# A Mamba-2 mixer blocked between token tiles, one decay matrix for both directions, and a new order of work

## What is computed

```python
def ssd_chunked(xs, dt, a_coef, bm, cm):          # 2 chunks of 128 tokens, 8 groups of 4 heads of 64
    a_cs = jnp.cumsum(a, axis=1)                  # a = dt * a_coef
    decay = exp(where(lower, a_cs[l] - a_cs[s], -inf))
    cb = einsum('clgn,csgn->clsg', cc, bc)
    y_diag = einsum('clsg,clsgk,csgkp->clgkp', cb, decay, xdt)
    ...                                           # the state carried from chunk to chunk gives y_off
y = y_fwd + y_bwd + d_skip[:, None] * xs          # y_bwd: the same on the flipped sequence
y = grouped_rmsnorm(y * silu(z)) @ w_out
```

## Time and profile before

| | |
|---|---|
| median of 3 runs | 1599.66 us (1599.23 to 1608.36) |
| the profiled execution | 1603.29 us, span 1601.5 us |
| mean granted TensorE clock | 0.968 |
| busy: PE, DVE, ACT, POOL | 94%, 63%, 48%, 18% |
| DMA | 275 MB at 172 GB/s |
| from the first matmul of the layer's own units to its last, SSD layer 0 | 13.45 to 307.95 us |
| the same, SSD layer 3 | 1113.4 to 1405.8 us |

### The profile page before, as it was taken

How to read it: one execution, slowest core, us unless ns; L and a number is a source line. 1 busy time by engine, 2 the same in 40 slices (tenths; PEclk the granted TensorE clock), 3 DMA queues, 4 the chain that set the end, 5 groups by cost and what they waited for, 6 DMA issues and landing times.

```text
span 1601.5 us, 25464 instructions
## 1 busy us (share of the span) xinstructions
PE 1510.0 (94%) x10189; PEld 1400.4 (87%) x10189; DVE 1007.5 (63%) x1123; ACT 769.8 (48%) x1079; POOL 288.1 (18%) x357
## 2 busy tenths in 40 slices
PE   6989999899998999999999999999989998899998
PEld 6989888699987989999899889998889998789996
DVE  4768886655467566545744465556778788565545
ACT  3566666344443334444355535442566766435441
POOL 1334443162220000000000000000244343200000
PEclk9989999999999999999999999999989999899999
DMA  8736753366766464555454246555665465336552
GB/s 252 213 118 177 198 191 134 106 178 195 224 199 203 143 202 138 181 208 189 160 192 140 84 132 210 194 175 169 199 206 171 146 199 167 122 106 205 187 187 79
DMA packets 200757, 275.43 MB, mean 172 GB/s; under 512 B 12280, under 2 KB 168336, under 8 KB 200640
## 3 DMA queue, kind: packets, MB, share of 16 engines
q1 hardware_dynamic: 188032, 237.53, 45.0%
q0 software_dynamic: 11760, 35.94, 8.3%
q10 hardware_dynamic: 848, 0.32, 0.1%
HBM read 272.58 MB, written 1.18 MB: 171 GB/s over the span
## 4 chain that ended last, share of the span: by engine, by line
PE 49%; DVE 8%; ACT 3%; issue 2%; POOL 1%; DMA 0%; DVEq 0%; ACTq 0%; POOLq 0%
PE y L680 20%; PE acc L556 17%; PE acc L569 6%; PE inner L816 3%; DVE conv L1461 2%; DVE w_low L1333 2%; ACT w_high L995 2%; PE y L569 1%; DVE E L1495 1%; ACT E L1089 0%; PE y L913 0%; DMA E<-cumsum_dram 0%; DVE xT L1394 0%; PE inner L646 0%; DVE gate L1510 0%
## 5 line engine op out<-in xcount | busy, mean ns | idle before, releaser
L556 PE MATMUL acc<-xT,w_high 128*128 128x256 f32 x3328 | 617.0, 287 | 3.5 <-DVE ring_c L1473 2.7
L1333 DVE TENSOR_TENSOR w_low<-raw,w_high 128x2048 fp32r<-128x2048 f32 x226 | 518.9, 2306 | 154.0 <-ACT w_high L995 136.0
L556 PEld LDWEIGHTS acc<-xT,w_high 128*128 128x128 f32 x3328 | 531.4, 195 | 10.3 <-DVE ring_c L1473 3.4
L995 ACT ACTIVATE w_high<-raw 128x2048 fp32r<-128x2048 f32 x226 | 426.8, 1897 | 214.1 <-PE y L680 78.5
L556 PE MATMUL acc<-xT,w_low 128*128 128x256 f32 x1664 | 475.0, 285 | 0.0
L680 PE MATMUL y<-w_high,opT 128*128 128x512 f32 x1408 | 404.0, 396 | 15.3 <-DVE opT L1481 12.2
L680 PEld LDWEIGHTS y<-w_high,opT 128*128 128x128 f32 x1408 | 262.4, 190 | 70.6 <-issue 19.3
L556 PEld LDWEIGHTS acc<-xT,w_low 128*128 128x128 f32 x1664 | 323.8, 195 | 0.0
L680 PE MATMUL y<-w_low,opT 128*128 128x512 f32 x704 | 225.0, 393 | 0.0
L1349 DVE TENSOR_TENSOR opT<-conv,opT 128x512 fp32r<-128x512 f32 x56 | 39.3, 702 | 270.5 <-issue 246.2
L569 PE MATMUL acc<-w_high,xT 128*128 128x256 f32 (+1 forms) x960 | 182.6, 292 | 9.8 <-DVE xT L1394 9.3
(11 more groups left out here) (168 smaller groups left out, 1212.6 us busy)
## 6 DMA issues: line engine op xcount, KB each, us to landing
raw<-in_ffn_w_in SPq DMA_DIRECT2D x128, 512.0 KB, 4.7
raw<-in_ffn_w_out SPq DMA_DIRECT2D x128, 512.0 KB, 4.5
raw<-in_ssd_w_in SPq DMA_DIRECT2D x96, 512.0 KB, 5.4
E<-cumsum_dram POOLq DMA_DIRECT2D x32, 512.0 KB, 5.9
raw<-in_ssd_w_out SPq DMA_DIRECT2D x32, 512.0 KB, 5.4
raw<-in_sc_w_in SPq DMA_DIRECT2D x24, 512.0 KB, 4.6
raw<-in_na_w_qkv SPq DMA_DIRECT2D x24, 512.0 KB, 4.6
E<-cumsum_dram POOLq DMA_DIRECT2D x32, 256.0 KB, 6.3
```

The costliest lines, as they stand in the source:

```text
L556: mm = nc.tensor.matmul(bank[:, c * SEQ:(c + 1) * SEQ][:, span], w[:, col:col + P], xT[:, k, low, span], start=(k == 0 and part == 0), sto ...
L995: nc.scalar.activation(w_high[:, u % SPLIT, 0:k * c], raw[:, u % RAW, 0:k * c], ACT.Copy).then_inc(w_high_done, 1)
L1333: V.tensor_tensor(w_low[:, u % SPLIT, 0:k * c], raw[:, u % RAW, 0:k * c], f(w_high[:, u % SPLIT, 0:k * c]), ALU.subtract).then_inc(w_low_d ...
```

## The change

Between the two token tiles nothing depends on the pair of tokens but the score: so the far block is now the plain score (copied by ACT, `copy_cross`) times x scaled by its decay to the tile's end (`scale_xs`), two matmuls of 256 columns a group (`cross_chunk`), and DVE multiplies the result by the decay from the end and adds it (`add_cross`). Within a tile, forward decay stands in one triangle and backward decay in the other of one matrix: ACT shifts the backward half by a bias (`shift_decays`, 8 instructions), DVE joins the triangles (`join_decays`), ACT takes 8 exponentials in place of 16, DVE multiplies once. dt goes into the exponent as its logarithm, so x isn't scaled for the scan, and the scan is 8 matmuls a group. The diagonal lacks one direction; DVE sums the scores' diagonal and makes a factor for x (`own_token`), which takes the skip along, and POOL multiplies (`own_xs`). The DMAs of E are two a group, the selects are gone.

The order is new on all engines: the scan of a group comes one iteration earlier on PE, `dt` is ahead of z, and the time constants are ahead of the first silu. In the convolution layer PE projects cc and ch for the first token tile before the second has come (`features` with 128 columns), and each output unit comes one step later. x is loaded ahead of the weights.

```diff
@@ -78,10 +79,10 @@
         names = {}
         if kind == "ssd":
             for g in range(G + 2):
+                if g == 0:
+                    add(names, "dt", j, 0)
                 if g < G - 1:
                     add(names, "z", j, g)
-                if g == 0:
-                    add(names, "dt", j, 0)
...
         elif kind == "conv":
-            for b in range(5):
-                if b < 4:
-                    for what in ("cc", "ch", "cb"):
-                        add(names, what, j, b)
-                if b >= 1:
-                    add(names, "co", j, b - 1)
+            for b in range(4):
+                for what in ("cc", "ch", "cb"):
+                    add(names, what, j, b)
+                if b == 2:
+                    add(names, "co", j, 0)
+            for b in range(1, 4):
+                add(names, "co", j, b)
...
         def ahead_of_norm(s, t):
-            if t and s + 1 < len(subs) and subs[s + 1][0] == "ssd":
+            if t and s + 1 < len(subs) and subs[s + 1][0] in ("ssd", "conv"):
...
         @block.sync
         def _(sp):
+            for t in range(NT):
+                sp.dma_start(xs[:, t, :], x[0, t * P:(t + 1) * P, :]).then_inc(x_landed[t], 16)
             for u in range(len(units)):
-                if u < NT:
-                    sp.dma_start(xs[:, u, :], x[0, u * P:(u + 1) * P, :]).then_inc(x_landed[u], 16)
...
-                    def mask_decays(g):
...
-                        for q, (off, sign) in enumerate(((0, 1), (256, -1), (384 + P, -1), (640, 1))):
-                            v = slot[:, :, off:off + P]
-                            ins = nc.gpsimd.affine_select(out=v, in_=v, compare_op=ALU.is_ge, fill=GONE, base=0,
-                                                          pattern=[[0, HPG], [sign, P]], channel_multiplier=-sign)
-                        ins.then_inc(e_masked, 1)
+                        for d in range(2):
+                            src = rows[d * HEADS + g * HPG:d * HEADS + (g + 1) * HPG, :]
+                            src = bass.AP(src.tensor, src.offset, [[0, P], [1, HPG * SEQ]])
+                            pool.dma_start(decay_slot(n)[:, d * HPG * SEQ:(d + 1) * HPG * SEQ], src).then_inc(e_landed[n % 2], 16)
...
+                    def own_xs(g):
                         n = first + g
-                        pool.wait_ge(xs_scaled, n + 1)
-                        times_heads(tri_b[:, n % 2, :], n, spread(skip[:, j, g * HPG:(g + 1) * HPG],
-                                                                  [[0, NT], [1, HPG], [0, HD]])).then_inc(xs_skip, 1)
+                        pool.wait_ge(own_done, n + 1)
+                        if n:
+                            pool.wait_ge(off_added, n)
+                        times_heads(xs_own, n, spread(own_token[:, n % 2, 0, :],
+                                                      [[HPG, NT], [1, HPG], [0, HD]])).then_inc(xs_skip, 1)
...
-                    for g in range(G - 1):
+                    pool.wait_ge(ends_done, first // G + 1)
+                    for g in range(G):
                         scale_xs(g)
-                        if g >= 1:
-                            rms_power(g - 1)
-                            load_decays(g + 1)
-                        skip_xs(g)
-                        if g >= 1:
-                            mask_decays(g + 1)
-                    scale_xs(G - 1)
-                    rms_power(G - 2)
-                    skip_xs(G - 1)
-                    rms_power(G - 1)
+                        own_xs(g)
+                        if g + 2 < G:
+                            load_decays(g + 2)
+                        rms_power(g)
...
-                    head_units(s, [names[("z", 0)], names[("dt", 0)]])
+                    head_units(s, [names[("dt", 0)], names[("z", 0)]])
...
+                    def cross_chunk(g):
+                        m = n0 + g
+                        pe.wait_ge(cb_copied, m + 1)
+                        pe.wait_ge(xs_scaled, m + 1)
+                        bank = inner_bank(("off", m), (off_scaled, m + 1))
+                        for t in range(NT):
+                            mm = nc.tensor.matmul(bank[:, t * GW:(t + 1) * GW], cross[m % 2][:, (1 - t) * P:(2 - t) * P],
+                                                  xs_end[:, (1 - t) * GW:(2 - t) * GW], start=True, stop=True)
+                        mm.then_inc(off_ready, 1)
...
-                                             (1, ((P, xs_fwd, c0), (640, xs_fwd, c1), (384 + P, xs_bwd, c1)))):
-                                for q, (c, v, cv) in enumerate(terms):
-                                    mm = nc.tensor.matmul(bank[:, t * GW + h * HD:t * GW + (h + 1) * HD],
-                                                          e[:, c:c + P], v[:, cv:cv + HD], start=(q == 0), stop=(q == 2))
+                            for t in range(NT):
+                                c = t * GW + h * HD
+                                mm = nc.tensor.matmul(bank[:, c:c + HD], decay_slot(m)[:, h * SEQ + t * P:h * SEQ + (t + 1) * P],
+                                                      tri_b[:, m % 2, c:c + HD], start=True, stop=True)
...
-                    for i in range(1, G - 1):
-                        project(names[("z", i)], range(NT))
-                        if i <= 2:
-                            project(names[("bc", i)], range(NT))
+                    for i in range(1, G):
+                        if i < G - 1:
+                            project(names[("z", i)], range(NT))
+                        state_products(i - 1)
                         turn_xs(i - 1)
-                        if i >= 2:
-                            scan(i - 2)
-                        state_products(i - 1)
-                        if i > 2:
-                            project(names[("bc", i)], range(NT))
-                        if i > 2:
-                            turn_gated(i - 2)
+                        project(names[("bc", i)], range(NT))
+                        cross_chunk(i - 1)
+                        scan(i - 1)
                         project(names[("x", i)], range(NT))
-                        if i == 2:
-                            turn_gated(i - 2)
-                        if i >= 2:
-                            out_unit(s, names[("so", i - 2)], first=(i == 2))
-                    project(names[("bc", G - 1)], range(NT))
-                    turn_xs(G - 2)
-                    scan(G - 3)
-                    state_products(G - 2)
-                    project(names[("x", G - 1)], range(NT))
-                    turn_gated(G - 3)
+                        if i < G - 1:
+                            if i >= 2:
+                                out_unit(s, names[("so", i - 2)], first=(i == 2))
+                            turn_gated(i - 1)
...
                 elif kind == "conv":
-                    head_units(s, [])
-                    for b in range(5):
-                        if b < 4:
-                            project(names[("cc", b)], range(NT), arriving=None if b else (s, NT - 1))
+                    head_units(s, [names[("cc", 0)], names[("ch", 0)]])
+                    for b in range(4):
+                        if b:
+                            project(names[("cc", b)], range(NT))
                             project(names[("ch", b)], range(NT))
-                            project(names[("cb", b)], range(NT))
-                        if 1 <= b < 3:
-                            out_unit(s, names[("co", b - 1)], first=(b == 1))
+                        project(names[("cb", b)], range(NT))
+                        if b >= 2:
+                            out_unit(s, names[("co", b - 2)], first=(b == 2))
...
+                    def shift_decays(g):
+                        m = n0 + g
+                        act.wait_ge(e_landed[m % 2], 32 * (m // 2 + 1))
+                        for h in range(HPG):
+                            for t in range(NT):
+                                c = HPG * SEQ + h * SEQ + t * P
+                                e = decay_slot(m)[:, c:c + P]
+                                ins = nc.scalar.activation(e, e, ACT.Identity, bias=apart[:, t, g * HPG + h:g * HPG + h + 1])
+                        ins.then_inc(e_shifted, 1)
...
+                            for t in range(NT):
+                                e = decay_slot(m)[:, h * SEQ + t * P:h * SEQ + (t + 1) * P]
+                                ins = nc.scalar.activation(e, e, ACT.Exp, bias=ncs[:, t, g * HPG + h:g * HPG + h + 1])
...
+                    def copy_cross(g):
+                        m = n0 + g
+                        act.wait_ge(cb_ready, m + 1)
...
+                    act.wait_ge(dt_floor, mixer + 1)
+                    nc.scalar.activation(dtt[:, 6, :, :], dtt[:, 7, :, :], ACT.Ln).then_inc(dt_log, 1)
+                    z_tanh(0)
...
+                    for i in range(1, G):
+                        if i < G - 1:
+                            z_tanh(i)
```

(81 more changed lines are left out.)

195 lines of the change are left out of this document (78 added, 117 removed).

## The result

The changed kernel takes 1647.4 us (median of 4, 1645.9 to 1648.5) where the kernel before takes 1599.5: ratio 1.0278, 95% interval 1.0247 to 1.0309. It is 2.8% slower. The forecast was 1614.0, 0.9% slower, with 1641 as its upper end: the direction was right, the size was not. The profiled executions have spans of 1644.6 and 1601.5 us, a difference of 43.1.

A forecast was written before the change was run, and what follows sets the result against it. A loop of hand-overs between PE, DVE and ACT bounds the SSD iteration: 31.8 us, 33.4 with the clock. 1601.5 + 2 x 9.0 (mixers) - 6 + 3 (convolution) - 2 (start) = 1614.5, taken as 1614.0 us; range 1578 to 1641.

The forecast's parts named there:

- The loop: SSD iteration: PE, DVE and ACT hand-overs through turn_xs's wait for gated_low and add_cross take 31.8 us, against 32.0 before.
- Rival 3: SSD iteration: splits are done in time, PE bounds it at 28.5 us without stall; kernel 1552 us, chance 0.15.
- The clock: SSD iteration: the slow clock behind PE's wait of about 4.2 us at turn_xs costs 1.6 us a group.
- The upper bound of 3.1: SSD iteration: the most that the slow clock behind the stall was taken to cost, 3.1 us a group.
- The end of the mixer: SSD mixer, from scan 6 through the last output unit: 43.2 us at full clock.
- The start of the mixer: SSD mixer: the first scan comes 10.5 us sooner.
- The convolution layer: Convolution layer: -6 us at its end, where co1 fills PE's stall, and +3 at its start.
- Rival 2: Convolution layer's start: matmuls of 128 columns run at the plain float32 rate, 220 ns; kernel 1634 us, chance 0.2.
- DVE and ACT even: SSD iteration: DVE's 1.5 us more a group offset by POOL's selects gone; ACT half a microsecond less.
- the start of the program: Layer 0: x loaded ahead of the weights and dt's smaller load save 2 us.

The follow-up runs named there:

- Run 1: Changed kernel with the gated operand's two instructions (ACT and DVE) ahead of the weight split in each steady iteration: 1593.9 us, 0.9973 of the kernel before.
- run 3: Changed kernel with extra, never-read matmuls on PE ahead of turn_xs, in the stall: 1622.7 us, 1.0127 of the kernel before.
- run 6: Changed kernel with the order of DVE and ACT in the SSD mixers written anew: 1547.6 us, 0.9652 of the kernel before.
- Run 11: Changed kernel with only the last gated operand of each SSD mixer put ahead of the last split: 1646.3 us, 1.0277 of the kernel before.
- Run 8: Kernel before with only the new convolution layer put in: 1599.0 us, 0.9972 of the kernel before.
- run 2: Changed kernel with the gated operand right behind start_conv of x on ACT and ahead of the taps of x on DVE: 1594.7 us, 0.9985.
- run 10: run 7 with instructions added on PE, DVE and ACT whose results are never read: 1588.3 us.
- run 7: run 6 with the counter of small PSUM results raised by 4 ahead of the attention layer: 1539.3 us, 0.9621 of the kernel before.

## Why the prediction was wrong in size and right in kind

Four steps of the sum failed: the price of the clock behind a stall, the end of the mixer, where the splits were left out, and two terms that it put at nothing, the attention layer and the end of the program. The loop itself was right.

**The loop** held. The odd number of small results, the wait at `turn_xs` for `gated_low`, and the loop through `add_cross` are in the trace, 4.20 us at each steady stall (9.93 and 7.45 at the last two). Run 1 shows the cause: with the operand ahead of the split the stall is 1.44 us and the iteration 30.3. Its sum of 31.8 us measured 31.5 in run 3. Rival 3, the broken loop, needed another order on ACT and DVE; run 6 shows it at 27.1 us.

**The clock** was the first mis-sized term. 1.6 us was taken from the earlier trace rows, the cheapest of three stalls; it measured 2.4. The length of the wait didn't tell the price: behind 4.26 us before the clock was at half for some 3.4 us (0.63 over 4 us and 0.95 over the next 4), behind 4.20 us here for 5.4. And the stall of 3.01 us was read too cheap: its window of 4 us ended before the clock was back, and the next 4 us (595 to 599, clock 0.77) lost 0.9 us more, so 2.9 and not 2.0. With 31.5 that gives the 33.9 us, against 33.4. The six iterations from the first scan to the seventh (1189.18 to 1393.30) took 204.1 us, 3.7 us a mixer more than forecast: 6 x 0.8 for the clock, less 6 x 0.3 for the loop, and 0.7 for iterations a little longer than 33.9. The upper bound of 3.1 held.

**The end of the mixer** was the second: 43.2 us from the seventh scan, and 1.6 for the clock, against 50.4. Three of its terms were short. Transposes to scan of group 7: 6.0 against 8.7 us, because half an output unit, at half clock, stands between `turn_xs` and the cross product. The gate to the operand: 6.5 against 9.3, because a split stands ahead of it on ACT and on DVE. The output unit: 5.5 against 7.3, at half clock behind another stall. DVE and PE, in order of time:

```profile
1433.11 2.29 DVE L1338 TENSOR_TENSOR w_low<-raw,w_high 128x2048 fp32r<-128x2048 f32 x1 [4.83 <-ACT w_high L997]
1435.32 0.87 DVE L1488 SCALAR_TENSOR_TENSOR opT<-inner,ssd_par,opT 128x256 fp32r<-128x256 f32 x2
```
```profile
1436.34 0.47 PE L681 MATMUL y<-w_high,opT 128*128 128x512 f32 x1 [3.01 <-DVE opT L1488]
```

The prediction had counted splits ahead of each hand-over in the loop and left them out in the tail. Together that is 5.6 us a mixer (7.3 for the three terms, less the 1.6 that the forecast had for the clock and 0.2 by which the way from the seventh scan to `turn_xs` was shorter: 25.0 against 25.2). Run 11 took 4.1 of it back to the last matmul, and 2.7 with the longer wait behind it.

**The start of the mixer** was right: 10.5 us sooner to the first scan in the forecast, 11.4 in the trace (66.65 us from the first projection in layer 3 before, 55.2 after). So layer 3's mixer came to +17.3 us: +9.0 forecast, 3.7 and 5.6 as above, less 0.9.

**The convolution layer** was right to 0.1 us in the changed kernel: -3 against -3.0. Run 8 shows it alone. But in five of the twelve profiled executions with the new layer the clock fell in it, and it took 116.2 us, which is 6.6 more than the kernel before; the forecast gave the wait of 1.07 us there no price in clock, and that the changed kernel's execution is not one of the five is luck. Rival 2, 220 ns for 128 columns, is out.

**DVE and ACT even** was a little too high: DVE's busy time is 23.96 us an iteration and ACT's 20.27 (25.36 and 21.55). The taps take 479 ns each on average, where they took 572 in the kernel before; that it is the selects on POOL that are gone no run shows by itself.

**What the sum didn't have.** The attention layer's 3.1 us: the change touches nothing there, but it adds 8 small results to a mixer, and the ring of six banks then starts two places further on, so that a transposed block lands in a bank that the output unit needs. The end of the span with 5.3 us, in POOL's closing DRAIN. And 1.0 us in MLP 0, where the first matmuls run at half clock. The forecast had put all three at nothing.

Sum: 1614.0, 2 x (3.7 + 5.6 - 0.9), 3.1, 5.3 and 1.0 make 1640.2. Of the remaining 7.2 us, 4.1 are layer 0's mixer: the forecast gave it 9.0 - 2.0 for the start of the program, with 8.4 as above 15.4, and it took 19.5. Of this 3.0 come from using layer 3's 225.7 us for both mixers: from the first scan to the end layer 0 took 222.75 before (85.20 to 307.95), and now both take 254.5 to 254.7. Another 1.0 is the start of the program: the first scan of layer 0 came 12.4 us sooner, 1.0 more than layer 3's, where the forecast took 2. The rest is that the median lies 2.8 us above the profiled span of 1644.6 where the forecast put it 0.5 below.

## What to carry to other kernels

Where small results rotate over a few buffers, count them modulo the number of buffers before changing their number: the change ties a result to a different predecessor, in later layers too. Work taken off the bounding engine is easily lost where a long, movable instruction (here a weight split of 2 us on two engines) stands ahead of a hand-over; put these where their engine waits anyway, then count. And price the last iteration from its own order, with every instruction that stands ahead of its hand-overs.

## What the runs showed of the hardware

How long the clock stays low isn't settled by the stall. Behind a wait of 1.69 us the output unit ran at 0.62 in the changed kernel and at 1.00 in run 1 (3.12 us of work). Behind the wait of 1.07 us in the convolution layer the profiled executions of runs 2, 3, 6, 10 and 11 ran at half clock for some 20 us and took 116.2 us for the layer, the others 106.6. No run here shows what decides between the two. Run 6 and run 7, the same work (window, then busy times and clock):

```profile
476.00:486.00 10.00, 10.00 (x57) 10.00 (x57) 4.49 (x2) 4.91 (x4) 0.00 (x0) 0.59 0.58 193
486.00:496.00 10.00, 10.00 (x49) 10.00 (x49) 4.30 (x6) 2.03 (x2) 0.00 (x0) 0.50 0.39 123
```
```profile
486.00:496.00 10.00, 10.00 (x87) 10.00 (x86) 7.46 (x10) 3.78 (x2) 0.00 (x0) 1.00 0.74 233
```

These 9.6 us may be most of what separates the executions of one kernel with the new convolution layer: run 3's four lie at 1616.4, 1617.7, 1627.7 and 1628.0 us, of which only the one at 1627.7 was profiled. The Trainium skill (TensorE: Matmul & The Clock Gate, Part 1) says that the number of matmuls at the low clock differs from run to run of one kernel. The profiles agree in kind; the 9.6 us are this case's own figure.
